# Hybrid decoder block with routed experts: first halves of two input projections between the row tiles, their weights split sooner, the vector rows loaded by ScalarE's queue

## What is computed

```python
def rmsnorm(x, g):
    xf = x.astype(jnp.float32)
    y = xf * lax.rsqrt(jnp.mean(xf * xf, axis=-1, keepdims=True) + RMS_EPS)
    return (y * g.astype(jnp.float32)).astype(x.dtype)

h = rmsnorm(x, norm_mix_g[l])
proj = h @ w_in[l]                       # 1024 x 1536
u_rnn, g_rnn, u_pool, q_mem = ...        # 512, 512, 256, 256 columns of proj
y_rnn = rg_lru(causal_depthwise_conv(u_rnn, conv_w[l], conv_b[l]), ...) * jax.nn.gelu(g_rnn)
y_mem = memory_cross_attention(q_mem, rmsnorm(mem, mem_norm_g[l]), w_mem_kv[l])
```

## Time and profile before

| | |
|---|---|
| median of 3 runs | 1741.6 us (1741.24, 1741.6, 1746.62) |
| profiled execution: its own time, its span | 1743.29 us, 1741.6 us |
| PE busy | 1667.9 us (96% of the span) |
| VectorE, ScalarE, POOL busy | 1303.3, 1103.9, 463.9 us |
| DMA | 485.64 MB, 279 GB/s over the span |

### The profile page before, as it was taken

The page is one execution under the profiler, slowest core; times in us unless marked ns, Lnnn a source line. Parts: engine busy times, 40 slices in busy tenths (PEclk is TensorE's granted clock), DMA queues, the critical chain, the costliest instruction groups (busy, mean ns, idle before and its releaser), DMA issues.

```text
span 1741.6 us, 29439 instructions
## 1 busy us (share of the span) xinstructions
PE 1667.9 (96%) x8641; PEld 1242.4 (71%) x8642; DVE 1303.3 (75%) x1168; ACT 1103.9 (63%) x1074; POOL 463.9 (27%) x348
## 2 busy tenths in 40 slices
PE   6999999759999999999999999999999999999996
PEld 6877777546786768888868887678666767765674
DVE  5578656666787868998869997669668669665787
ACT  5455555355676758877758876567556657654674
POOL 5000002432322525322225222215213026123240
PEclk9999999869999999999999999999999999999998
DMA  9121132467898989999989998689868788887685
GB/s 281 52 97 58 52 110 73 170 237 288 329 346 326 350 316 350 389 380 385 391 321 351 390 375 324 232 347 378 307 263 296 299 326 324 296 319 259 227 324 218
DMA packets 114171, 485.64 MB, mean 279 GB/s; under 512 B 16430, under 2 KB 29040, under 8 KB 81360
## 3 DMA queue, kind: packets, MB, share of 16 engines
q1 hardware_dynamic: 96128, 445.58, 66.0%
q0 software_dynamic: 18000, 39.49, 9.3%
HBM read 451.79 MB, written 33.23 MB: 278 GB/s over the span
## 4 chain that ended last, share of the span: by engine, by line
PE 71%; DVE 3%; issue 2%; DMA 2%; ACT 1%; POOLq 0%; ACTq 0%; DVEq 0%; POOL 0%; SPq 0%
PE ps L1837 20%; PE ps L1839 18%; PE ps L1838 18%; PE ps L1852 6%; PE ps L1890 3%; DVE w_lo L1681 2%; PE ps L1810 2%; PE ps L1860 1%; DMA raw_weights<-in_w_down 1%; ACT w_hi L1535 1%; PE ps L1915 1%; DVE raw_weights L1782 0%; PE ps L1819 0%; DMA stand_in<-token_lists 0%; DVE raw_weights L1799 0%
## 5 line engine op out<-in xcount | busy, mean ns | idle before, releaser
L1681 DVE TENSOR_TENSOR w_lo<-raw_weights,w_hi 128x2048 fp32r<-128x2048 f32 x256 | 576.5, 2284 | 137.8 <-ACT w_hi L1535 137.8
L1535 ACT ACTIVATE w_hi<-raw_weights 128x2048 fp32r<-128x2048 f32 x256 | 485.5, 1911 | 219.7 <-DMA raw_weights<-in_w_gu 114.9
L1837 PE MATMUL ps<-w_hi,xT 128*128 128x512 f32 x1024 | 415.4, 406 | 10.7 <-issue 5.1
L1838 PE MATMUL ps<-w_lo,xT 128*128 128x512 f32 x1024 | 402.9, 393 | 0.0
L1839 PE MATMUL ps<-w_hi,xT 128*128 128x512 f32 x1024 | 402.4, 393 | 0.0
L1681 DVE TENSOR_TENSOR w_lo<-raw_more,w_hi 128x2048 fp32r<-128x2048 f32 x128 | 290.1, 2284 | 28.8 <-ACT w_hi L1535 28.2
L1837 PEld LDWEIGHTS ps<-w_hi,xT 128*128 128x128 f32 x1024 | 194.1, 190 | 91.4 <-issue 46.6
L1535 ACT ACTIVATE w_hi<-raw_more 128x2048 fp32r<-128x2048 f32 x128 | 244.2, 1908 | 0.3 <-DMA raw_more<-in_w_down 0.3
L1461 POOL DMA_INDIRECT x_rows<-h_rows,next_list x33 | 79.0, 2395 | 598.0 <-issue 598.0
L1839 PEld LDWEIGHTS ps<-w_hi,xT 128*128 128x128 f32 x1024 | 193.8, 189 | 42.7
L1838 PEld LDWEIGHTS ps<-w_lo,xT 128*128 128x128 f32 x1024 | 194.3, 190 | 36.7
(11 more groups left out here) (318 smaller groups left out, 2134.9 us busy)
## 6 DMA issues: line engine op xcount, KB each, us to landing
raw_weights<-in_w_gu SPq DMA_DIRECT2D x192, 1024.0 KB
raw_more<-in_w_gu SPq DMA_DIRECT2D x64, 1024.0 KB, 6.7
raw_weights<-in_w_down SPq DMA_DIRECT2D x64, 1024.0 KB
raw_more<-in_w_down SPq DMA_DIRECT2D x64, 1024.0 KB, 11.6
rows<-in_x SPq DMA_DIRECT2D x12, 512.0 KB
w_in_sb<-in_w_in SPq DMA_DIRECT2D x12, 512.0 KB, 4.6
acc_rows<-region_c SPq DMA_DIRECT2D x8, 512.0 KB
h_rows<-region_c SPq DMA_DIRECT2D x8, 512.0 KB
```

The source lines that it names most:

```text
L1535: S.activation(w_hi[:, j % RING, :], raw(j % RING), ACT.Copy).then_inc(hi_done, 1)
L1681: V.tensor_tensor(w_lo[:, j % RING, :], raw(j % RING), w_hi[:, j % RING, :].bitcast(F32), ALU.subtract).then_inc(lo_done, 1)
L1837: T.matmul(out, hi, hi_w, start=first, stop=False)
L1838: T.matmul(out, hi, lo_w, start=False, stop=False)
```

## The change

- Between the row tiles, behind tile 4, PE now runs a quarter (two k-blocks, six matmuls) of projection 0 half 0, and so behind tiles 5, 6 and 7; behind tiles 8 and 9 half of projection 1 half 0 each (twelve matmuls). Behind tile 9 follow projection 0 half 1 and projection 1 half 1. The four halves hence finish in another order, which the new `projected(n, h)` gives to all that wait for `proj_ready`.
- The vector rows are issued by ScalarE, ahead of its first square, transposed ahead of tile 1 and copied by VectorE in step 1.
- w_in_hi(0), w_in_hi(1) stand in ScalarE's steps 3 and 5, w_in_lo(0), w_in_lo(1) in VectorE's steps 4 and 6.
- SP issues w_in(0) behind row tile 3 and w_in(1) behind row tile 6, both without a wait, and w_in(2) behind the last row tile.

```diff
+        def projected(n, h):
+            return 2 * n + h + 1 if n >= 2 else 2 * h + n + 1
...
-            for item in range(len(row_slots)):
+            for item in range(TT // 2):
                 load_rows(item)
-            for n in range(3):
-                load_w_in(n)
-                sp.wait_ge(xT_ready, n + 1)
-                load_rows(len(row_slots) + n)
+            load_w_in(0)
+            for item in range(TT // 2, len(row_slots)):
+                load_rows(item)
+            load_w_in(1)
+            for item in range(len(row_slots), NORMED):
+                sp.wait_ge(xT_ready, item - len(row_slots) + 1)
+                load_rows(item)
+            load_w_in(2)
...
-            for r, n, src in vector_rows:
-                pool.dma_start(vrows[r:r + n, :], src).then_inc(vrows_in, 16)
...
             act.preload_act_table(ACT.Sqrt)
+            act.wait_ge(pool_step, 3)
+            for r, n, src in vector_rows:
+                act.dma_start(vrows[r:r + n, :], src).then_inc(vrows_in, 16)
             square(0)
...
-                if s == 5 or s == 7:
-                    w_in_hi((s - 5) // 2)
+                if s == 3 or s == 5:
+                    w_in_hi((s - 3) // 2)
...
-                if s == 3:
+                if s == 1:
                     vector_columns()
...
-                if s == 6 or s == 8:
-                    w_in_lo((s - 6) // 2)
+                if s == 4 or s == 6:
+                    w_in_lo((s - 4) // 2)
...
+            first_parts = {TT // 2: (0, 0, 2), TT // 2 + 1: (0, 2, 4), TT // 2 + 2: (0, 4, 6), TT // 2 + 3: (0, 6, 8),
+                           TT: (1, 0, 4), TT + 1: (1, 4, 8)}
             for s in range(NORMED):
-                if s == 2:
+                if s == 1:
                     pe.wait_ge(vrows_in, 16 * 8)
                     T.transpose(bank(0)[:, 0, 0:V_N], vrows[0:V_N, :], ident[0:V_N, 0:V_N]).then_inc(vecT_ready, 1)
                 transpose_rows(s)
-                if s >= TT - 1 and s < NORMED - 1:
-                    project_half(0, s - TT + 1)
+                if s in first_parts:
+                    n, k, stop = first_parts[s]
+                    project_half(n, 0, range(k, stop))
+            project_half(0, 1)
+            project_half(1, 1)
...
             for c in range(RT):
                 if c:
                     project(2 * c)
-                project(2 * c + 1)
-                if c == 0:
+                    project(2 * c + 1)
+                else:
                     keys_values()
                 gates(c)
```

More of the change, by code:

```diff
@@ L455, in w_in_hi @@
                 elif n >= 2:
-                    act.wait_ge(proj_ready, 2 * (n - 1))
+                    act.wait_ge(proj_ready, max(projected(n - 2, h) for h in range(2)))
                 nc.scalar.activation(w_in_parts(n)[0], w_in_sb[:, n % 3, :, :], ACT.Copy).then_inc(w_in_hi_done, 1)
+            vector_rows = [
+                (V_CONVW, CONV * RT, dram["conv_w"][0].rearrange("w (c p) -> (w c) p", p=P)),
+                (V_CONVB, RT, dram["conv_b"][0].rearrange("(c p) -> c p", p=P)),
+                (V_BA, RT, dram["b_rg_a"][0].rearrange("(c p) -> c p", p=P)),
+                (V_BI, RT, dram["b_rg_i"][0].rearrange("(c p) -> c p", p=P)),
+                (V_LAM, RT, dram["lru_lambda"][0].rearrange("(c p) -> c p", p=P)),
+                (V_PS, PT_, dram["pool_scale"][0].rearrange("(c p) -> c p", p=P)),
+                (V_GMIX, KT, dram["norm_mix_g"][0].rearrange("(c p) -> c p", p=P)),
+                (V_GMEM, KT, dram["mem_norm_g"][0].rearrange("(c p) -> c p", p=P)),
+            ]
             act.preload_act_table(ACT.Sqrt)
+            act.wait_ge(pool_step, 3)
+            for r, n, src in vector_rows:
+                act.dma_start(vrows[r:r + n, :], src).then_inc(vrows_in, 16)
             square(0)
@@ L484, in u_evac @@
                 for h in range(2):
-                    act.wait_ge(proj_ready, 4 * c + h + 1)
+                    act.wait_ge(proj_ready, projected(2 * c, h))
                     nc.scalar.activation(u_pad[:, PAD + h * HALF:PAD + (h + 1) * HALF], bank(2 * ((2 * c) % 2) + h)[:, 0, :],
@@ L494, in g_evac @@
                 for h in range(2):
-                    act.wait_ge(proj_ready, 4 * c + 2 + h + 1)
+                    act.wait_ge(proj_ready, projected(2 * c + 1, h))
                     nc.scalar.activation(g_t[:, h * HALF:(h + 1) * HALF], bank(2 + h)[:, 0, :],
```

## The result

The changed kernel took **1756.4 us** (median of 4 runs, 1755.88 to 1756.84), the kernel before, run beside it, 1742.8 (4 runs, 1741.24 to 1746.62). The ratio is 1.0078, with a 95% interval from 1.0063 to 1.0094: **0.8% slower**, where I had forecast no difference (1743.7, range 1740.0 to 1746.0), and over the 5.2 us bound. The forecast was wrong.

The account below looks back on a forecast made before the run. PE alone was taken to set the pace from 31.4 us on, other engines before. Closed holes, a 1.9 us stall and tile 4's 0.15 us gave +0.4, the clock +1.7: +2.1 us, 1743.7 us, range 1740.0 to 1746.0.

Parts of the forecast that it names:

- 5.2 us bound: Whole kernel: 0.3% of its time, about what a measurement can tell from no change.
- All behind starts later by what PE lost: After the projections: everything later shifts by PE's loss, +0.4 + 1.7 = +2.1 us, with no further cost.
- Start, eight DMA issues on ScalarE: Before the first square: issues take 3.6 us, square(0) comes 1.48 us late, covered by square(2)'s 1.75 us wait; cost 0.
- Rival B: ScalarE's issues cost over 0.48 us each, delaying tile 0; 1745.4; sign: square(2) follows square(1) without a wait; chance 0.10.
- Loads, vector rows: Row tiles and w_in in new order arrive in time; the small transpose fits the 0.76 us before tile 2; cost 0.
- rival D: Vector rows land late, so PE waits for them behind tile 0; 3.9 us more, 1747.6; chance 0.08.
- The stall: Behind tile 4, PE's first projection part waits for w_in_lo(0) from 24.05 to 25.95: 1.9 us.
- Tile 4's slip: Tile 4 starts at 22.05 instead of 21.90, as scale(4) comes later: 0.15 us.
- The clock: Behind the new PE pause the granted clock falls below 1.00 between 25 and 30 us, costing a further 1.7 us.
- rival A: The pause behind tile 4 comes without a fall of the clock: +0.4 us, 1742.0; chance 0.28.
- Rival C: No wait behind tile 4, since w_in_lo(0) is done when tile 4 ends: -1.5 us, 1740.1; chance 0.12.
- if the time moves while its start does not: Sign of a wrong forecast: the kernel's time changes though keys_values does not start at another moment.

Follow-up runs that it names:

- e3: Kernel before with only the eight vector rows issued by ScalarE instead of POOL; 1742.47 us, ratio 0.9997.
- e8: Changed kernel, repeated waits dropped, TensorE's program at its old length, first projection part behind tile 5 instead of tile 4; 1738.11 us, ratio 0.9990.
- e2: Changed kernel with repeated waits dropped and satisfied ones added, so TensorE's code stands where it did before; 1741.55 us, ratio 0.9996.
- e5: Kernel before with one more instruction (two satisfied waits) at the head of TensorE's program; 1754.21 us, ratio 1.0077.
- e1: Kernel before with three more instructions (six satisfied waits) at the head of TensorE's program; 1757.36 us, ratio 1.0081.
- e4: Changed kernel with 253 more idle instructions at the head of TensorE's program, its loop 256 places behind that of before; 1763.14 us, ratio 1.0117.
- e7: Kernel before with 64 more instructions (128 satisfied waits) at the head of TensorE's program; 1749.32 us, ratio 1.0051.

## Why the prediction was wrong

- **"All behind starts later by what PE lost": the step that failed.** The sum ended at keys_values and carried its +2.1 us on unchanged. Behind that point the changed kernel lost 15.1 us by itself, as the same matmuls waited for code. No rival named it: all four were about the first 60 us. The diff held what was needed to ask: the parts repeat their waits, TensorE's program gets three instructions longer, and I costed them at nothing without saying so. The trace of before held it too: the 1.93 us pause at 464.25, which I took as a specimen for the clock, comes of a wait for code, with "issue" as its label. The sequencer's branch at 458.1 took 3.84 us, a packet of code starting at 459.6 within it, while queued matmuls ran on; with that lead gone, its branches and register loads of the next unit (461.98 to 464.24) left TensorE idle.
- **Start, eight DMA issues on ScalarE: cost 0, right, at a smaller price.** The timeline of ScalarE after:

```profile
0.97 1.28 ACT L465 ACT_TABLE_LOAD   x1 [0.84 <-PEq L2041]
1.49 0.40 ACTq L468 DMA_DIRECT2D vrows<-in_conv_w  x1
...
4.26 0.32 ACTq L468 DMA_DIRECT2D vrows<-in_mem_norm_g  x1
4.62 1.06 ACT L425 ACTIVATE region_c<-rows 128x1024 f32<-128x1024 f32 x1 [2.37 <-DMA rows<-in_x]
...
7.24 1.06 ACT L425 ACTIVATE region_c<-rows 128x1024 f32<-128x1024 f32 x1
```

  Eight take (4.26 + 0.32 - 1.49) = 3.09 us, 0.39 each (0.45 taken), and they begin under the table load, not behind it. Square(0) comes at 4.62 rather than at my 5.85. Square(2), at 7.24, no longer waits for its row, which was B's sign, but not for B's cause: its row was there at least 1.3 us sooner than the 8.61 of before, and ScalarE, at less than B's 0.48 us a piece, ran its squares without a pause. So that sign didn't tell the two apart. Rival B has no ground, and e3 measures this part at no difference.
- **Loads, vector rows: cost 0, right.** The small transpose stands at 12.60 us, behind tile 0 and without a wait; rival D didn't come.
- **The stall: right in place and cause, 1.68 us instead of 1.9.** Tile 4's slip, 0.15: from tile 0 to tile 4 it is 11.76 us against 11.61. Tiles 5 and 6 followed without a hole, as forecast. A tile with a part of six matmuls takes 29.09 - 25.92 = 3.17 us, not 3.4, since a tile inside a dense stream takes 27.62 - 25.92 = 1.70. So the stage ends 0.2 us sooner relative to tile 0, not 0.4 later.
- **The clock: wrong, rival A right.** Behind the stall:

```profile
24.40:26.40 2.00, 1.99 (x11) 1.72 (x12) 1.97 (x7) 1.33 (x4) 1.83 (x6) 1.00 1.02 363
```

  The granted clock stays at 1.00, the 2.4 GHz level, so the +1.7 us of the sum were nothing. A pause of 1.68 us didn't lower it here, one of 1.93 had before; I chose by nearness between two rows, and a duration alone doesn't settle it. The sign that I wrote down for a wrong forecast, "if the time moves while its start does not", is what happened.
- **Rival C** needed the stall to stay out; e8 takes it out, and gives 1.35 us against before where C had 1.5.

As a statement on the edit's own work the forecast without the clock's fall, +0.4 us, isn't contradicted: e2, the same work with the loop in its place, is 0.2 us below before, with an interval of about 3 us to either side.

## What to carry to other kernels

Where an engine runs a long loop with branches, count the instructions that an edit adds **ahead** of the loop on that engine, even satisfied waits: the loop's code moves with them, and three of them cost 0.8% here, 1,300 us later. Before judging an edit by its time, compare the idle time ahead of the loop's first matmuls and the length of the sequencer's branches with those of the kernel before (the packets of the code queue alone missed e5), and run the edit once at the old length of the program and the old kernel once at the new: the pair e1 and e2 parted work and place in two runs. A wait whose label says "issue", or names an engine that had long been done, at a branch, is a candidate for code.

## What the runs showed of the hardware that I had not expected

- The same loop of TensorE, 1,707 instructions, ran from 470 to 1110 us without one packet on the code queue. Three places further on it took 14 packets from 1125 to 1700 us, with waits of up to 6.5 us. The Trainium skill (Runtime: NRT & Kernel Launch, Instruction fetch mechanics) says that a taken branch can force a fetch, and the long branches (2.5 to 6.2 us in the changed kernel, against at most 0.3 us for the branch back otherwise) agree. The same three instructions are worth 14 to 16 us ahead of the loop and nothing behind it.
- One instruction over a block's end is enough: in e5 the loop's last branch came up to 5.93 us late, with no packet more than before.
- A long wait for code costs more than its length, since the clock falls behind it: nine matmuls in 4 us at 0.50 after the 6.47 us.
- A satisfied wait is not free: 254 of them in a row took TensorE 0.108 us each (e4). Sixty-four (e7) cost nothing at the start, where TensorE waits for its first tile anyway: 46.63 us from tile 0 to keys_values, and tile 0 at 9.05.
- ScalarE issues a DMA in 0.39 us, and begins while its table load still runs (1.49 us against the load's end at 2.25).
